# Three, then four weight buffers; seven, then six gather buffers; and another order of the query units in a Mamba-2 / PEER layer

## The reference

```
h2 = modulate(rmsnorm(x), shift, scale)                       # (512, 1024)
q  = (h2 @ w_q).reshape(T, 8 heads, 2 sides, 128)             # w_q is 1024 x 2048
s  = einsum('thpd,hpnd->thpn', q, keys)                       # 128 scores a side
sv, si = top_k(s, 16)                                         # per side
cv, ci = top_k(all 16 x 16 sums of the two sides, 16)
eid = i1 * 128 + i2                                           # 16 experts a head, 128 a token
g  = softmax(cv)
u  = u_tab[eid];  act = gelu(einsum('thkd,td->thk', u, x))
y  = einsum('thk,thkd->td', g * act, v_tab[eid])
out = x + gate * rmsnorm(y)
```

## Time and profile before

| | |
|---|---|
| three runs, us | 2083.15, 2076.49, 2072.24 |
| median, us | 2076.49 |
| profiled execution, us | 2083.15 (span 2081.4) |
| busy: PE, DVE, ACT, POOL | 72%, 72%, 24%, 43% |
| mean granted TensorE clock | 0.853 |
| moved | 647.28 MB, 555.78 MB of it through the gathers' queue |

### The profile page before, as it was taken

The page is one execution under the profiler, slowest core; times in us unless marked ns, Lnnn a source line. Parts: engine busy times, 40 slices in busy tenths (PEclk is TensorE's granted clock), DMA queues, the critical chain, the costliest instruction groups (busy, mean ns, idle before and its releaser), DMA issues.

```text
span 2081.4 us, 15935 instructions
## 1 busy us (share of the span) xinstructions
PE 1506.1 (72%) x4648; PEld 873.3 (42%) x4648; DVE 1489.0 (72%) x2906; ACT 498.3 (24%) x1413; POOL 885.5 (43%) x658
## 2 busy tenths in 40 slices
PE   7799999889757788887965677765555556556554
PEld 3465787668535455664631345411111111111111
DVE  2545358764246567887789967498898898998976
ACT  2200120101122233222233232223222223222222
POOL 2468403220013333343335534356555555555553
PEclk9899899989889889998986899877768787677777
DMA  8233212114249899999999999799999999999997
GB/s 330 100 124 141 100 64 77 63 61 148 95 192 353 350 355 337 416 420 377 419 412 340 422 371 370 300 407 409 423 421 422 417 420 403 414 422 421 407 422 292
DMA packets 90604, 647.28 MB, mean 311 GB/s; under 512 B 10413, under 2 KB 10773, under 8 KB 12565
## 3 DMA queue, kind: packets, MB, share of 16 engines
q0 software_dynamic: 76448, 555.78, 66.4%
q1 hardware_dynamic: 13376, 90.25, 11.3%
q10 hardware_dynamic: 693, 0.23, 0.0%
HBM read 644.12 MB, written 2.10 MB: 310 GB/s over the span
## 4 chain that ended last, share of the span: by engine, by line
PE 39%; DVE 25%; DMA 21%; issue 8%; ACT 6%; POOL 1%; SPq 0%; DVEq 0%; ACTq 0%; POOLq 0%
DMA arena<-in_peer_uv,arena 19%; PE bank L672 12%; PE bank L918 8%; DVE arena L1643 8%; DVE arena L1658 6%; PE bank L888 6%; PE bank L857 4%; PE bank L708 3%; ACT arena L1134 1%; ACT smalls L1139 1%; POOL arena L614 1%; ACT arena L1129 1%; PE bank L907 1%; DVE arena L1234 1%; PE bank L698 1%
## 5 line engine op out<-in xcount | busy, mean ns | idle before, releaser
L614 POOL DMA_INDIRECT arena<-in_peer_uv,arena x512 | 695.8, 1359 | 882.0 <-DVE arena L1658 525.2
L918 PE MATMUL bank<-arena,smalls 128*128 128x512 f32 x1024 | 686.3, 807 | 469.4 <-ACT smalls L1139 469.4
L1643 DVE CUSTOM_DVE_ANT_0 arena<-arena 128x1024 f32<-128x1024 f32 x512 | 613.0, 1221 | 59.1 <-DMA arena<-in_peer_uv,arena 57.3
L918 PEld LDWEIGHTS bank<-arena,smalls 128*128 128x128 f32 x1024 | 222.1, 237 | 871.1 <-ACT smalls L1139 675.2
L1658 DVE SCALAR_TENSOR_TENSOR arena<-arena 128x1024 f32<-128x1024 f32 x252 | 322.0, 1278 | 199.2 <-ACT arena L1134 199.2
L672 PE MATMUL bank<-arena 128*128 128x256 f32 (+1 forms) x1216 | 337.6, 435 | 3.5 <-ACT arena L963 3.2
L672 PEld LDWEIGHTS bank<-arena 128*128 128x128 f32 x1216 | 237.1, 196 | 104.7 <-issue 76.0
L1129 ACT ACTIVATE arena<-arena 128x2 f32<-128x2 f32 x256 | 51.9, 203 | 763.3 <-DVE arena L1643 761.8
L888 PE MATMUL bank<-arena 128*128 128x256 f32 x512 | 128.3, 409 | 19.1 <-issue 16.3
L888 PEld LDWEIGHTS bank<-arena 128*128 128x128 f32 x512 | 107.8, 211 | 53.1 <-issue 34.8
L1134 ACT ACTIVATE arena<-arena 128x1 f32<-128x1 f32 x512 | 122.9, 287 | 8.5
(11 more groups left out here) (241 smaller groups left out, 1306.6 us busy)
## 6 DMA issues: line engine op xcount, KB each, us to landing
arena<-in_w_in SPq DMA_DIRECT2D x40, 1024.0 KB, 6.1
arena<-in_w_ada POOLq DMA_DIRECT2D x16, 1024.0 KB, 5.1
arena<-in_w_out SPq DMA_DIRECT2D x16, 1024.0 KB, 7.2
arena<-in_peer_w_q SPq DMA_DIRECT2D x16, 1024.0 KB, 8.5
arena<-in_w_ada SPq DMA_DIRECT2D x8, 1024.0 KB, 7.8
arena<-in_peer_uv,arena POOLq DMA_INDIRECT x512, 10.6
arena<-in_x SPq DMA_DIRECT2D x4, 512.0 KB, 9.2
out<-arena SPq DMA_DIRECT2D x4, 512.0 KB, 8.0
```

Of the source, the lines that this page charges most:

```text
L614: nc.gpsimd.indirect_dma_start(gslot[n % NGS], None, uv_tab[0], bass.IndirectOffsetOnAxis(eid[t % 2][:, k:k + 1], 0)).then_inc(s_gsl[n % N ...
L918: last = mm(acc[h][:, :], diag[:, j % NDG], row_v(n)[:, h * 512:(h + 1) * 512], start=(i == 0), stop=(i == BT - 1))
L1643: V.tensor_tensor_reduce(row_u(n), row_u(n), h2[t], 1.0, 0.0, ALU.mult, ALU.add, dots[:, k:k + 1]).then_inc(s_dot, 1)
```

## The change

The weight ring gets a fourth buffer, in the 8 KB a partition that were the first of the seven gather buffers; six of these stay. The units change their order inside each half: before, both tiles took a quarter of `w_q` in turn, (0,0) (1,0) (0,1) (1,1) and so on, written as (tile, quarter); now each tile takes two quarters, (0,0) (0,1) (1,0) (1,1), then (0,2) (0,3) (1,2) (1,3). Two units, not three, run ahead of pick 0, and the transposes of tile 1 stand behind the second. The steps of the third unit go to the head of `side`, which is 3 entries longer up to `late`; the second half of the units still begins at entry 88. With an even number of gather buffers the gather n and the one that it replaces have the same parity, so the wait of POOL tests n.

```diff
-    WRING = 3
+    WRING = 4
...
-    units = [(2 * tp + i, 2 * qh + k) for tp in range(2) for qh in range(QB // 2) for k in range(2) for i in range(2)]
+    units = [(2 * tp + i, 2 * qh + k) for tp in range(2) for qh in range(QB // 2) for i in range(2) for k in range(2)]
...
-    side = [s for u in units[3:NUA] for s in unit_steps(u)]
+    side = [s for u in units[2:NUA] for s in unit_steps(u)]
...
-    BSEQ += [("h2T", 1)] + sum(unit_steps(units[1]) + unit_steps(units[2]), [])
+    BSEQ += sum(unit_steps(units[1]), []) + [("h2T", 1)]
...
-        gslot = [at(k, 2 * D) for k in (24, 56, 64, 72, 80, 88, 96)]
+        gslot = [at(k, 2 * D) for k in (56, 64, 72, 80, 88, 96)]
...
                 if n >= NGS:
-                    last = n - NGS
-                    if last % 2:
-                        pool.wait_ge(s_peused, last // 2 + 1)
+                    if n % 2:
+                        pool.wait_ge(s_peused, (n - NGS) // 2 + 1)
                     else:
-                        pool.wait_ge(s_vadd, last // 2 + 1)
+                        pool.wait_ge(s_vadd, (n - NGS) // 2 + 1)
```

## The result

The changed kernel is slower: 2092.94 us in the median of 6 runs, against 2081.72 of 6 runs of the kernel before beside it. The ratio is taken from more runs (25 of the changed kernel, median 2095.89) and is 1.0065, 95% interval 1.004 to 1.0091, so 8 to 19 us. The forecast was 2067, in a range up to 2086. The profiled execution has a span of 2089.7 us, against 2081.4.

A forecast was written before the change was run, and what follows sets the result against it. The gathers' bytes were taken to set the pace of most picks. Terms -21.0 + 20.3 - 14.9 + 5.0 + 1 + 2 - 2 = -9.6 gave 2067 us against the median of 2076.49, range 2054 to 2086.

The forecast's parts named there:

- Step 1: Start of the picks: second unit's matmuls run under the ranking, pick 0 at 598.1 instead of 619.1: -21.0 us.
- Step 2: Picks beside units, first half: three more picks have a unit's step beside them, at a cycle of 20.3 us: +20.3.
- Step 3: Bare picks before entry 88: three fewer, 12 or 13 become 9 or 10, at 4.98 us each: -14.9.
- Step 4: After both chain-bound stretches: with six buffers the reserve of landed rows is one gather less, 2.5 us each: +5.0.
- step 6: Late stretch: a gather buffer less where weight pieces share the engines with gathers: +2, bounds 0 and 12.
- rival C: Late stretch: weights crowd out gathers, its 12 us and the reserve's 5 come together: about 0, 2077; chance 0.20.
- Step 7: Start of the kernel: with four weight buffers token tiles from the third on issue one step earlier: -2, bounds 0 and -3.8.
- Step 5: Bare stretches: a gather buffer less comes out of queueing, the queue stays filled, only lumps are lost: +1, bounds 0 and 6.
- Rival B: Bare stretches: with six buffers the engines run empty between gathers, slower, +21, so 2098; decides from 0.06 us a gather; chance 0.11.
- signs of being wrong: Bare picks over 5.15 us, DMA share there below 0.98, late over 405 us, new `w_q` wait, or POOL's hole unchanged.
- sign of being right: Last tiles: gathers' landing with a median near 8.8 at a rate still of 417 GB/s; one of several signs.
- Step 8: Second half's units: the fourth weight buffer elsewhere and the new unit order change nothing: 0.

The follow-up runs named there:

- the ring alone: The kernel before with six gather buffers instead of seven and nothing else changed: 2106.97 us, ratio 1.0121.
- grown rings: The changed kernel with weight buffers joining the gather ring from gather 228 on: ten buffers 2074.14 us, ratio 0.9955; seven 2079.78 us, ratio 0.9992.
- Growing to seven: The changed kernel with one buffer more, seven, from gather 228 on: 2079.78 us, ratio 0.9992.

## Why the prediction was wrong, step by step

**Step 1, pick 0 earlier: right.** -21.0 said. From the transposes of tile 0 (559.44, then 557.43) to pick 0 it is 59.7, then 39.5 us: -20.2. The missing 0.8 lies in the transposes and scores at the clock of 0.50. This part repeats: 58.1 to 59.8 us in the seven profiles with the old order, 39.5 to 39.6 in the seven with the new one.

**Step 2, a unit more: right**, +20.3 said, +20.0 measured. **Step 3, fewer bare picks: right**, -14.9 said, -13.7 measured.

**Step 4, the reserve, and step 6, the late stretch: right in the late part.** +4.5 said, +4.4 measured; the experiments give 4 to 5 to the six buffers. The fourth weight buffer, about 1 us there, has next to no price of its own (rival C). The Trainium skill's rule of queues served in turn ("DMA: Bandwidth & Descriptors", section "Queues, rings and completion order") is not contradicted by this: bytes that go to weights early are not moved later.

**Step 7, the start: wrong.** -2 said. After the change:

```profile
3.97 0.57 SPq L495 DMA_DIRECT2D arena<-in_w_ada  x1
...
20.72 0.43 SPq L488 DMA_DIRECT2D arena<-in_ctx  x1
...
32.40 1.06 ACT L949 ACTIVATE arena<-arena 128x1024 f32<-128x1024 f32 x1 [27.24 <-DMA arena<-in_ctx]
```

The fourth piece goes out at 3.97, the last tile 3.0 us earlier, but the squares begin only 0.8 earlier than in the earlier trace rows. The first h2 transposes come 2.0 earlier, but that is luck of this pair: they stand anywhere from 556.8 to 563.5 in the profiles here. Over all of them the squares begin at 32.6 us in the mean with three weight buffers (six profiles) and at 32.1 with four (eight), the transposes at 558.6 and at 559.9. So the start gains half a us, and nothing of it is seen at the transposes. The near match of the table's first line, -22.2 for -23.0, owes 2 us to this luck.

**Step 5, six buffers in the bare stretches: this is what failed.** "I take +1, bounds 0 and 6"; with the half of term 4 that was 3.5 us. It measured +17.4, and +20.6 with the ring alone, of which some 3 may be term 4's. The mechanism was named (lumps of DVE work, rival B), but the step held that "the queue stays filled", since the shortest landing of 8.8 us less 2.5 is still above 5.5. The 5.5 is one gather that finds nothing in its way. Six and five buffers show that a stream is already thin when gathers still take over 8: 8.4 in the median at 346 GB/s. It stood in the earlier trace rows too, 8.0 in the median beside the units, where the earlier trace rows shows the engines at 0.91. By 8.0 the margin of the shortest landing was 0.8 with seven buffers and none with six. The landings of the four rings say the same: the median ends at 8.4 to 8.9 and not at 5.5. Why it ends there is not shown; that a gather shares the engines with its neighbour, released within a few us, and so needs 5.5 + 2.5 = 8.0, is an estimate that fits. Rival B was the right one, at half of its price and with a chance of 0.11; its point of decision, 0.06 us a gather, was reached: 17.4 / 286 = 0.06.

The signs of being wrong were set on two measures, and only one spoke. Bare picks came out at 737.0 / 143 = 5.15 us, the bound that was named. The DMA share stayed at 1.00, far from the 0.98, while the rate fell from 417 to 409 GB/s. And the first half of a sign of being right was met: with six buffers alone the median landing is 8.9 us, "near 8.8", but at 406 GB/s and not at 417. The rate is what must be read.

**Step 8**: the unit order in the second half stayed without effect that can be told: +2.3 in the changed kernel, 0.0 and -1.5 in its variants with grown rings.

Growing to seven restores the stretch, 720.0 against 719.6. The sum without that stretch's 3.5 is -13.1 us. The profile of that kernel gives -8.2, but its runs give 0.9992 (0.9968 to 1.0017) of before, so 2 us and at most 7. Step 5 is then the larger part of the miss and not all of it; the rest lies ahead of pick 112, where pick 0 comes 17.6 us earlier in the mean and not 23.0. That part stays within the scatter of single profiles, and its cause is open.

## What to carry to other kernels

A ring of buffers for a stream that sets the pace has a knee, and the last buffer above it looks free: seven was about 3 us from the floor, six about 20, five 150. Its margin is not to be read against the landing time of a lone transfer, but against that in a stretch of the same profile where the stream is just no longer full. And a buffer that is traded away for one phase can be given back when the other user is done; this brought both gains together.

## What the runs showed of the hardware

With half of the matmuls per pick TensorE's granted clock was 0.50 in the whole stretch, against 0.73 with all of them, so that its part of a pick took 2.1 us for half of the work and 3.0 for all of it. The same 12 picks took 89.4 to 90.5 us at a clock of 0.88 or 0.89, and 82.1 to 83.8 at 0.97 to 1.00, in different kernels: with two kernels that differ by a few us, a single profile of that stretch decides nothing. And a stream of 1 MiB gathers ran at 421, 417, 406 and 346 GB/s with rings of ten, seven, six and five buffers.
